# Modulation in a decoder trunk: chunks taken in pairs in the values, one product for each pair

## The reference

```python
c_act = jax.nn.silu(c)
ada = c_act @ w_ada[layer] + b_ada[layer]            # 1024 x 6144, for each of two layers
sh1, sc1, g1, sh2, sc2, g2 = jnp.split(ada, 6, axis=-1)
h = ada_modulate(x, norm_mix_gain[layer], sh1, sc1)
proj = h @ w_in                                      # retention: q, k (1024 each), v, gate g (2048 each)
shift, scale = jnp.split(c_act @ kv_w_ada + kv_b_ada, 2, axis=-1)   # for the shared keys and values
```

## Time and profile before

| | |
|---|---|
| median of 3 runs | 2933.74 us (2933.66 to 2935.83) |
| the profiled execution | 2935.14 us, its span 2933.6 us |
| mean granted clock of TensorE | 0.993 |
| TensorE busy | 2875.6 us (98%) |
| VectorE busy | 1829.9 us (62%) |
| ScalarE busy | 1045.3 us (36%) |
| loads of modulation tiles by SyncE (L613) | 80 from w_ada and 16 from kv_w_ada, 0.5 MB each |

### The profile page before, as it was taken

How to read it: one execution, slowest core, us unless ns; L and a number is a source line. 1 busy time by engine, 2 the same in 40 slices (tenths; PEclk the granted TensorE clock), 3 DMA queues, 4 the chain that set the end, 5 groups by cost and what they waited for, 6 DMA issues and landing times.

```text
span 2933.6 us, 32929 instructions
## 1 busy us (share of the span) xinstructions
PE 2875.6 (98%) x12724; PEld 2318.9 (79%) x12724; DVE 1829.9 (62%) x2261; ACT 1045.3 (36%) x1341; POOL 337.5 (12%) x486
## 2 busy tenths in 40 slices
PE   6999999999999999999999999999999999999999
PEld 5878888777777888888888787866766888888887
DVE  7676567655557877686855254245454887767673
ACT  5211133322234333333335344334244433333331
POOL 0000000100002000111120010123121100011110
PEclk8999999999999999999999999999999999999999
DMA  7567556753313444654412323455352254475441
GB/s 241 184 225 251 189 172 206 267 189 105 119 37 104 170 143 150 250 202 144 137 43 101 122 87 130 140 130 123 81 118 80 98 172 158 154 260 177 136 137 58
DMA packets 193134, 439.49 MB, mean 150 GB/s; under 512 B 13105, under 2 KB 83172, under 8 KB 192996
## 3 DMA queue, kind: packets, MB, share of 16 engines
q0 software_dynamic: 61616, 222.34, 22.8%
q1 hardware_dynamic: 131380, 215.27, 22.3%
HBM read 314.09 MB, written 123.34 MB: 149 GB/s over the span
## 4 chain that ended last, share of the span: by engine, by line
PE 89%; DVE 5%; ACT 2%; DMA 2%; issue 1%; POOL 0%; SPq 0%; DVEq 0%; ACTq 0%; POOLq 0%
PE ps L2695 8%; PE ps L2697 8%; PE ps L2696 8%; PE ps L2866 6%; PE ps L2868 6%; PE ps L2864 6%; PE ps L2996 4%; PE ps L2492 4%; PE ps L2491 4%; PE ps L2488 4%; PE ps L2621 3%; PE ps L2625 3%; PE ps L2624 3%; PE ps L2448 3%; PE ps L2451 2%; PE ps L2454 2%
## 5 line engine op out<-in xcount | busy, mean ns | idle before, releaser
L2864 PE MATMUL ps<-z_hi,w_hi 128*128 128x512 f32 x768 | 298.8, 389 | 0.0
L2866 PE MATMUL ps<-z_lo,w_hi 128*128 128x512 f32 x768 | 298.8, 389 | 0.0
L2868 PE MATMUL ps<-z_hi,w_lo 128*128 128x512 f32 x768 | 298.8, 389 | 0.0
L2695 PE MATMUL ps<-h_hi,w_hi 128*128 128x512 f32 x576 | 224.4, 390 | 0.0
L2697 PE MATMUL ps<-h_hi,w_lo 128*128 128x512 f32 x576 | 224.1, 389 | 0.0
L2696 PE MATMUL ps<-h_lo,w_hi 128*128 128x512 f32 x576 | 224.1, 389 | 0.0
L2488 PE MATMUL ps<-z_hi,w_hi 128*128 128x512 f32 x512 | 203.5, 397 | 0.0
L2492 PE MATMUL ps<-z_hi,w_lo 128*128 128x512 f32 x512 | 199.4, 389 | 0.0
L2491 PE MATMUL ps<-z_lo,w_hi 128*128 128x512 f32 x512 | 199.2, 389 | 0.0
L1895 DVE SCALAR_TENSOR_TENSOR xT<-ps,ada,xT 128x512 f32<-128x512 f32 x128 | 93.9, 749 | 147.4 <-PE ps L2492 147.4
L1566 DVE TENSOR_TENSOR w_lo<-w_raw,w_hi 128x2048 fp32r<-128x2048 f32 x52 | 118.8, 2285 | 107.4 <-ACT w_hi L1025 107.4
(11 more groups left out here) (398 smaller groups left out, 6635.9 us busy)
## 6 DMA issues: line engine op xcount, KB each, us to landing
t_s<-misc POOLq DMA_DIRECT2D x28, 1792.0 KB, 6.9
misc<-t_s POOLq DMA_DIRECT2D x98, 512.0 KB, 4.2
misc<-w_ada SPq DMA_DIRECT2D x84, 512.0 KB, 4.7
w_raw<-w_mlp_in SPq DMA_DIRECT2D x32, 1024.0 KB, 5.4
w_raw<-ret_w_in SPq DMA_DIRECT2D x24, 1024.0 KB, 7.7
x_s<-xT SPq DMA_DIRECT2D x12, 1024.0 KB, 6.1
xT<-x_s SPq DMA_DIRECT2D x12, 1024.0 KB, 12.3
a_bufs<-w_mlp_out SPq DMA_DIRECT2D x12, 1024.0 KB, 22.5
```

The lines of the kernel that those rows point to most:

```text
L2695: MM(out, hi, b_hi[:, k, :], start=k == 0 and i in (0, 1, 3), stop=False, skip_group_check=True)
L2864: MM(bank[at + m], hi, ring_b(z_hi, slot)[:, cols], start=first and i not in (2, 4, 5), stop=False, skip_group_check=True)
L2866: MM(bank[at + m], hi, ring_b(z_lo, slot)[:, cols], start=False, stop=False, skip_group_check=True)
L2868: mm = MM(bank[at + m], lo, ring_b(z_hi, slot)[:, cols], start=False, stop=last, skip_group_check=True)
```

## The change

The two slots stay, the loads and products are dealt out differently. Chunk 3 moves from the second trip of the keys to the third, and half of chunk 4 is the fourth's. The four trips of the values take the other half of 4 and chunk 5, then 6 and 7, 8 and 9, 10 and 11: a pair of chunks per trip, turned into two halves of ada_lanes and summed by one product of 64 columns. The gates take chunks 12 and 13, a quarter of a chunk per product. SyncE's queue follows that order; its loops and TensorE's loop over the value trips are written out. `ada_lanes` now lies in low_tiles. The core of the diff:

```diff
+ADA_GROUPS = ((2,), (3,), (4, 5), (6, 7), (8, 9), (10, 11), (12,), (13,))
...
+        ada_slot = [n % 2 for n in range(96)]
+        ada_held = [n - 2 if n > 1 else None for n in range(96)]
+        ada_count = [16 * (n // 2) + 16 for n in range(96)]
...
-            body(W_QK, [in_pair(ret_w_in, 512 + 256 * j) for j in range(2)], 2, w_ada[0], 2048, True)
-            with sp.Fori(1, 3) as i:
-                body(i * 2 + W_QK, [in_pair(ret_w_in, i * 512 + 512 + 256 * j) for j in range(2)],
-                     i + 2, w_ada[0], i * 1024 + 2048)
...
+            key_pair(2)
+            key_pair(3)
+            ada_loads(2, 0, 4)
+            key_pair(4)
+            ada_loads(2, 4, 8)
+            key_pair(5)
+            key_pair(6)
+            ada_loads(3, 0, 4)
+            key_pair(7)
+            ada_loads(3, 4, 8)
+            value_pair(W_V)
+            ada_loads(4, 0, 2)
+            value_pair(W_V + 1)
             for n in range(4):
                 sp.dma_start(x_quarter(n // 2, n % 2), xT[quarter(n // 2, n % 2)]).then_inc(x_moved[n], 16)
+            ada_loads(4, 2, 8)
+            for i in range(3):
+                value_pair(W_V + 2 * i + 2)
+                ada_loads(5 + 2 * i, 0, 4)
+                value_pair(W_V + 2 * i + 3)
+                ada_loads(5 + 2 * i, 4, 8)
+                ada_loads(6 + 2 * i, 0, 2)
+                if i < 2:
+                    ada_loads(6 + 2 * i, 2, 8)
...
+            ada_loads(10, 2, 8)
+            ada_loads(11, 0, 4)
+            load_gate(0)
+            load_gate(1)
+            ada_loads(11, 4, 8)
...
                 if k == 0:
+                    dve.wait_ge(ada_turned, chunk - 1)
                     ins = TS(ada_acc, raw, c_act[:, 0:1], None, ALU.mult)
...
             def rotary(unit, j):
                 dve.wait_ge(a_free, unit + (A_QK + j + 2))
+                if unit + j:
+                    dve.wait_ge(rot_done, (unit + j) // 2)
...
+            def third_trip():
+                prep(W_QK + 5, 1)
+                ada_tiles(3, 0, 6)
+                rotary(8, 0)
+                prep(W_QK + 6, 0)
+                ada_tiles(3, 6, 8)
+                rotary(8, 2)
+
+            def fourth_trip():
+                prep(W_QK + 7, 1)
+                rotary(12, 0)
+                ada_lane_columns(1)
+                prep(W_V, 0)
+                ada_tiles(4, 0, 4)
+                rotary(12, 2)
...
             def v_trip(i):
                 prep(i * 2 + (W_V + 1), 1)
-                for k in range(KT):
-                    ada_tile(i + 6, k)
+                ada_tiles(4 + 2 * i, 0 if i else 4, 8)
+                ada_tiles(5 + 2 * i, 0, 4)
                 if i < 3:
                     prep(i * 2 + (W_V + 2), 0)
+                ada_tiles(5 + 2 * i, 4, 8)
...
-                for k in range(4 * (q % 2), 4 * (q % 2) + 2):
-                    ada_tile(chunk, k)
+                ada_tiles(12 + q // 4, q % 4 * 2, q % 4 * 2 + 2)
...
+            def ada_sums(g, ada_ps=ada_ps):
+                width = 32 * len(ADA_GROUPS[g])
+                pe.wait_ge(ada_turned, ADA_GROUPS[g][-1])
+                pe.wait_ge(ada_read, g + 2)
+                MM(ada_ps[:, 0:width], lane_sum[:], ada_lanes[:, 0:width], start=True, stop=True,
...
-            with pe.Fori(0, 4) as i:
-                pe.wait_ge(ada_read, i + 6)
-                v_unit(i, W_V, A_V, V_ORDER, lambda: ada_sums(i + 6, ada_ps=ada_ps_v))
+            for i in range(4):
+                pe.wait_ge(ada_read, i + 4)
+                v_unit(i, W_V, A_V, V_ORDER, lambda: ada_sums(2 + i, ada_ps=ada_ps_v))
```

More of the change, by code:

```diff
@@ L605, in half_pair, with ada_load, ada_loads @@
                 return w[j * 512:(j + 1) * 512, bass.ds(col, 512)].rearrange("(k p) n -> p k n", p=P)
-            def ada_load(chunk, k, w, col):
-                if isinstance(chunk, int) and chunk == 2 and k < 2:
+            def ada_load(chunk, k):
+                n = (chunk - 2) * 8 + k
+                if ada_held[n] is None:
                     sp.wait_ge(columns_full, 4)
-                else:
-                    sp.wait_ge(ada_acc_done, chunk * 8 + (k - 17))
-                sp.dma_start(ada_raw[:, k % 2, :], w[k * P:(k + 1) * P, bass.ds(col, 1024)])\
-                  .then_inc(ada_loaded[k % 2], 16)
+                    if ada_slot[n] == 3:
+                        sp.wait_ge(angle_ready, 1)
+                else:
+                    sp.wait_ge(ada_acc_done, ada_held[n] + 1)
+                w = kv_w_ada if chunk >= 12 else w_ada[chunk // 6]
+                col = chunk % 6 * 1024
+                sp.dma_start(ada_ring[ada_slot[n]], w[k * P:(k + 1) * P, col:col + 1024]).then_inc(ada_loaded[ada_slot[n]], 16)
+            def ada_loads(chunk, first, last):
+                for k in range(first, last):
+                    ada_load(chunk, k)
             def load_slab(g):
@@ L634, in _, with key_pair, value_pair @@
             load_slab(3)
[L636 to L645, removed]
[L646 to L649 removed]
+            def key_pair(p):
+                load_pair(p, p % 2, in_pair(ret_w_in, 256 * p))
+            def value_pair(p):
+                load_pair(p, p % 2, half_pair(ret_w_in, p % 2, 2048 + (p - W_V) // 2 * 512))
             def x_quarter(hf, kh):
                 return x_s[4 * kh:4 * kh + 4, :, half(hf)].rearrange("k p n -> p k n")
[L652 removed]
+            key_pair(2)
[11 more added lines that the diff above has]
+            value_pair(W_V + 1)
             for n in range(4):
                 sp.dma_start(x_quarter(n // 2, n % 2), xT[quarter(n // 2, n % 2)]).then_inc(x_moved[n], 16)
[L655 to L657 removed]
+            ada_loads(4, 2, 8)
[7 more added lines that the diff above has]
+                    ada_loads(6 + 2 * i, 2, 8)
             def load_gate(q):
@@ L1585, in ada_turn, with ada_tiles, ada_lane_columns @@
                 dve.wait_ge(ada_acc_done, chunk * 8 - 8)
[L1586 to L1592, removed]
+                at = [group.index(chunk) for group in ADA_GROUPS if chunk in group][0]
+                nc.vector.tensor_reduce(ada_lanes[:, 32 * at:32 * at + 32], ada_acc.rearrange("p (b n) -> p b n", n=32),
+                                        AX.X, ALU.add, apply_transpose=True).then_inc(ada_turned, 1)
+            def ada_tiles(chunk, first, last):
+                for k in range(first, last):
+                    ada_tile(chunk, k)
+            def ada_lane_columns(g, src=ada_ps):
+                dve.wait_ge(ada_ps_done, g + 1)
+                cols = slice(ADA_GROUPS[g][0] * 8, ADA_GROUPS[g][-1] * 8 + 8)
                 for a in range(4):
                     rows = slice(32 * a, 32 * a + 32)
-                    ins = TT(ada[rows, cols], src[rows, a:32:4], bias_a[rows, cols], ALU.add)
+                    ins = TT(ada[rows, cols], src[rows, a:32 * len(ADA_GROUPS[g]):4], bias_a[rows, cols], ALU.add)
                 ins.then_inc(ada_read, 1)
@@ L1757, in first_trip @@
                 rotary(0, 0)
-                for k in range(3):
-                    ada_tile(2, k)
+                ada_tiles(2, 0, 3)
                 rotary(0, 2)
@@ L1763, in second_trip @@
                 prep(W_QK + 3, 1)
-                for k in range(3, KT):
-                    ada_tile(2, k)
+                ada_tiles(2, 3, 8)
                 rotary(4, 0)
                 prep(W_QK + 4, 0)
[L1768 to L1772, removed]
-                rotary(4, 2)
[L1775 to L1785, removed]
+                rotary(4, 2)
+                ada_lane_columns(0)
+            def third_trip():
[12 more added lines that the diff above has]
+                rotary(12, 2)
             first_trip()
             second_trip()
-            qk_trip(2, before=lambda: ada_lane_columns(3))
-            qk_trip(3)
+            third_trip()
+            fourth_trip()
             def gate_t_sums(i):
@@ L1874, in _ @@
                     gate_low(q + 1, 0)
-                if q and q % 2 == 0:
-                    ada_lane_columns(chunk - 1, ada_ps_g)
-                for k in range(4 * (q % 2), 4 * (q % 2) + 2):
-                    ada_tile(chunk, k)
+                if q == 4:
+                    ada_lane_columns(6, ada_ps_g)
+                ada_tiles(12 + q // 4, q % 4 * 2, q % 4 * 2 + 2)
                 if q + 1 < NG:
@@ L1884, in _ @@
                     gate_low(q + 1, 2)
-                for k in range(4 * (q % 2) + 2, 4 * (q % 2) + 4):
-                    ada_tile(chunk, k)
             prep(W_RET, 0)
-            ada_lane_columns(13, ada_ps_g)
+            ada_lane_columns(7, ada_ps_g)
             def add_job(d_job, q, gate, ring):
```

55 lines of the change are left out of this document (19 added, 36 removed).

## The result

| | before | after |
|---|---|---|
| median | 2933.70 us (2930.33 to 2935.83, 4 runs) | 2980.86 us (2980.23 to 2982.74, 4 runs) |
| the profiled execution | 2935.14 us | 2982.74 us |
| mean granted clock of TensorE | 0.993 | 0.987 |

The changed kernel takes 1.0162 times as long, 95% interval 1.0149 to 1.0175: 47.2 us more, where + 37.4 us were forecast. The two profiled executions differ by 47.6 us in span.

What follows compares the result with a forecast made beforehand. TensorE carries 89% of the chain of waits, so only its waits count. Gates 45.5 us late, less 3.9 and 4.2 us, gave + 37.4 us on 2935.1 us profiled, 2971 us as median; range 2945 to 2996 us.

Steps and rivals of the forecast that it cites:

- Keys: In the keys, both long TensorE waits, their clock loss and two products go: 9.6 us saved, values starting at 225.6 us.
- The tile step: In the values, VectorE starts a modulation tile every 3.0 us, paced by loads into two slots.
- The first pair's turn: First values trip: the first pair of chunks is turned at 268.8 us, so TensorE waits 5 us for it.
- Every further trip: Later values trips take 58.0 us, not 43.8, with TensorE waiting some 12 us before each pair's product; the last ends later.
- the formula: Length of a further values trip: 12.55 us in front, 0.85, 14 tile steps, then 2.55 for last tile and turn.
- Into the gates: Seam from values to gates: last values trip ends at 456.0 us, so the gates start 45.5 us late.
- Gates: In the gates, three trips with a modulation product become one, its chunk turned earlier: 3.9 us come back.
- The end: Behind the gates, two fewer tile loads and the mostly vanished rv_first wait with its clock loss save 4.2 us.
- VectorE's idle time: In the values, VectorE stands idle for loads some 85 us in all, given as four times 14 steps of 1.7.
- The loads are hidden: Rival: VectorE's idle time in the values is free, trips stay 43.8 us, total 2916 us; 5 in 100.
- Even: Rival: gain and loss meet at 2.3 to 2.4 us a values tile, time within the bound; 6 in 100.
- Dearer waits: Rival: spills stretch values tile steps beyond 3.25 us, + 50 us and more, 2984 us up; 15 in 100.

Runs made afterwards that it cites:

- before_ring4: Kernel before, a chunk per trip, with four ring slots up to chunk 9 and two from chunk 10 on; 2923.55 us, ratio 0.9967 to the kernel before.
- ring4: Changed kernel with four ring slots instead of two in keys and values, two again from chunk 12; 2922.25 us, ratio 0.9957 to the kernel before.
- ring3: Changed kernel with three ring slots instead of two in keys and values, two again from chunk 12; 2937.47 us, ratio 1.0015 to the kernel before.
- quarter_load: Changed kernel, two slots, each modulation tile's load bringing 128 KB instead of 512 KB, VectorE's work kept; 2925.09 us, ratio 0.9974 to the kernel before.

## Why the prediction was right, and where its sizes were off

The prediction had the sign, the place and the mechanism. Step by step:

**Keys: 9.6 us, measured 9.3.** The last evacuation of the keys that VectorE's rotary waits for is at 224.80 on ScalarE, against 234.13 before:

```profile
224.80 1.03 ACT L1094 ACTIVATE stage<-ps 128x1024 f32<-128x1024 f32 x1 [9.85 <-PE ps L2472]
```

No wait at the product between 125 and 230 us, as said.

**The tile step: 3.0 us, measured 3.44 in the first trip and 3.15, 3.09 and 3.13 in the others.** This is the mis-sized term. The prediction took it from six steps of the kernel before, 2.93 us in the mean, and from the median load of 4.6 us, and said itself that no row shows the added loads in the company they would have. Where they meet it the steps are long: of the second trip's 14 steps the two in which a weight load and spills of v_s run beside the tile loads take 5.54 and 5.49 us and the other twelve 33.1 us, 2.76 each, about what (4.3 + 1.28) / 2 gives. With small weight loads the three trips fall to 2.85 to 2.89 us. More care with the rows would have helped little: all 24 such steps in the four trips of the kernel before have a mean of 3.05 us. In that kernel the tiles of the second trip end at 303.7 us and its spills begin at 307.77; in the changed one the tiles go on to 332 us and meet them.

**The first pair's turn: 268.8, measured 273.5 (+ 4.7).** Ten steps of 0.44 us too little, and the first of these tiles 0.3 us later. It was TensorE's first wait, 10.8 us where 5 were forecast.

**Every further trip: 58.0, 58.0 and 60.2 us, measured 59.9, 59.8 and 62.1 (+ 1.9, + 1.8, + 1.9).** The parts in front of the tiles came out as forecast: with 3.15 us a step the formula gives 60.05 us. The waits were 14.0, 13.4 and 15.6 us for "some 12", and one of 2.4 us for the columns (L2640).

**Into the gates: 456.0, measured 45.5 + 11.4 = 56.9 us after the old start (+ 1.1 us at the seam itself).** ScalarE's L1195 waits 14.5 us for the gate sum with four evacuations queued behind it (457.21 and 458.17), as the prediction had it. The clock took 3.0 us of work here where 1.7 were forecast, which is the size of the error at this seam.

**Gates: - 3.9 us, measured - 3.8** (133.0 us from the first to the last spill, 136.9 before). The spills are 19.0 us apart. The one trip with a product shows 19.3 us (547.14 to 566.45), where 20.4 was forecast for it less 0.3 for the chunk turned earlier: a product alone costs 0.3 us. Of the rest, 1.1 us, its wait had been 0.8 us; the granted clock stayed at 1.00 behind such a wait (from 453 to 460 us of the kernel before), so what the last 0.3 us were is not shown.

**The end: - 4.2 us, not confirmed.** From the last spill to the end of the span took 2363.6 us before and 2358.1 after, 5.5 us less, and the wait for rv_first is gone. But `before_ring4` keeps that wait, 2.8 us, and took 2919.9 - 561.57 = 2358.3 us. Over the nine profiles of the other kernels this stretch lies between 2356.5 and 2361.5 us. So what the missing wait gives is within what executions differ by, and a wait of 2.0 us for k_tok has come up further on. This term was made of the wait's 1.7 us of clock and of 2.5 us for two loads fewer, which no row shows; the runs give it no support.

**VectorE's idle time: some 85 us, measured 89.0.** The count in brackets is wrong: four times 14 steps of 1.7 us are 95. The first trip has only ten steps, and 52 steps of 1.7 are 88.

**The errors together:** 4.7 + 1.9 + 1.8 + 1.9 + 1.1 = 11.4 us of late gates, + 0.1 in the gates, less 1.3 at the end: 10.2 us, the distance between 47.6 and 37.4.

**The rivals.** "The loads are hidden" is what `ring4` is: with steps that TensorE covers the kernel takes 2922 us, 6 us above the 2916 of the prediction; that rival failed on the two slots, not on its arithmetic. "Even" needed 2.3 to 2.4 us a tile; `ring3` had 2.24 in its second trip and came out at + 0.15%. "Dearer waits", steps beyond 3.25 us, held for the first trip only, but in the first three trips the loads do meet the spills, beside a weight load, and the two steps of each that do take 4.2 to 6.0 us. That rival was wrong in the mean, not in kind.

The fit of the Trainium skill, "DMA: Bandwidth & Descriptors", section "Anatomy of one DMA", is an estimate of 3.2 us a load and 2931 us by the prediction; with 4.3 us in the median and 2981 us the trace disagrees, as it did before the change. (By the prediction's own 52 us for each us of step, a step of 2.25 us gives 2932 rather than 2931 us.) The section states the fit for transfers issued by GpSimd; the prediction left that out, and these loads are SyncE's. Whether that or the other traffic makes the difference is not shown. For 128 KB the fit gives an estimate of 2.3 us, and `quarter_load` has 2.1 us.

**Open:** what makes a load longer with more requests in flight (4.3, 5.2, 6.3 us), how the excess of the long steps divides between weight loads and spills, and how much of the end's 5.5 us is the change.

## What to carry to other kernels

An engine that is idle for half of a stretch is not room for more work until its timeline says what the idle time is: if a load ends it, count steps of (load + use) / slots, and ask which weight loads and which spills of other queues the new steps will meet, before moving work there. If the steps don't fit, deepen the ring first: with two more rows of memory the kernel came out some 10 us faster than the kernel before in the new order of work, and some 9 in the old. Where a wait is ascribed to "issue", compare its end with the ends of the other engines' instructions: three of four were VectorE's turn to within 0.1 us. In the fourth the engine that the view named was the right one.

## What the runs showed of the hardware that was not expected

A load's time was no constant: the median of 0.5 MB was 4.3 us with two slots, 5.2 with three and 6.3 with four, while the kernel got faster. Removing 0.8 us of VectorE's work per tile shortened a step by 0.2 us instead of 0.4. A quarter of the bytes took half of the time (2.1 against 4.3 us). A load need not stand behind a large one to suffer: issued 0.4 us ahead of a weight load and beside a spill of v_s, one took 7.5 us. And what the clock costs at a seam did not go by the length of the wait: the granted clock stood at 0.50, the level of 1.2 GHz, for some 3 to 6 us after TensorE started again, and cost 1.7, 2.5, 1.6 and 3.0 us of work after waits of 10.8, 14.0, 13.4 and 15.6 us. After the wait of 3.0 us in the keys before it cost 1.7 us, and after waits of 0.8 us in the gates nothing.
